# A fused RWKV-7 / RG-LRU / mixture-of-experts layer on one core: another order at the start of a scan pass, and smaller transfers

## The chip, the cores and the metric

The kernel runs on one core of a Trainium2 chip. The metric is the device time of one execution in microseconds (us). A TensorE matmul and its weight load appear in the profile as PE and PEld; DVE is VectorE, ACT ScalarE, POOL GpSimd and SP SyncE.

## The reference

One layer of a diffusion backbone on 2048 latent tokens and 256 context tokens of width 1024. After a modulated norm and one input projection, two mixers run in both directions over the tokens: a gated linear recurrence (RG-LRU) and the RWKV-7 recurrence with 8 heads of 64, whose step is

```python
sa = jnp.einsum('bhvk,bhk->bhv', s, -kk_t)
s = (s * w_t[:, :, None, :] + sa[..., None] * (kk_t * a_t)[:, :, None, :]
     + v_t[..., None] * k_t[:, :, None, :])
return s, jnp.einsum('bhvk,bhk->bhv', s, r_t)
```

Their outputs are merged and projected, and a mixture of 16 experts and a last norm follow. The change touches only the stage that computes the two recurrences.

## The kernel before

The kernel is a row of stages: `entry` and `inward` (norm, input projection, operands of the recurrences), `scan` (both recurrences), `blend`, `outward`, `choose`, `experts`, `final`. In fp32 they each write their results to scratch tensors in DRAM.

`scan` works through 18 passes of 128 positions per direction in 64-wide chunks. Two units `u` (0 and 1) of 128 partitions each carry the heads, both directions `d` side by side. A pass of the RWKV recurrence has two parts. The *solve* (argument `a`) forms, for all chunks of pass `it`, the products of the operands and inverts a triangular matrix by five levels of squaring. The *state* part (argument `c`) carries the state S through the four chunks of the pass before, chunk by chunk in steps X, Z, S and Y. `body(a, c)` interleaves both on every engine in a fixed order: five steps `begin0` to `begin4`, then for each level m a step F and a step W; `STATE_AT` says which state step stands behind which solve step (X of chunk 0 behind `begin0`, Z0 behind `begin1`, S0 and Y0 behind `begin2`, X1 behind `begin3`, Z1 behind `begin4`, S1 and Y1 behind F1, and so on). There is no scheduler: each engine runs its queue in this order, and semaphores (`Steps`: one per engine and unit, counted by name) hold it where it needs another's result.

The five steps of the solve before the change, on PE: `begin0` makes L and its transpose Lt for both units, from `ob` and `aq` (L2273), into PSUM banks 2 and 3. `begin1` and `begin2` are `joint`: products B of one unit and K of the other at once (L2288), into the same banks. `begin3` transposes operands, tB, and V, out of `ob` and `over`, with an identity; `begin4` does tK. ACT copies L, tB, V and tK out of PSUM (L2430, L2433, L2435, L2438); DVE masks Lt into T (L2599) and B and K into W, Lb, La and Lk, a direction at a time (L2607); POOL adds units to T and W (`start_solve`, L2774) and masks L into the tiles H of the levels (`level`, L2784). F1 multiplies H with W.

The same queues carry the RG-LRU, a piece of 256 positions per chunk: ACT's `gates` behind X, at Z the `squares` and, at chunk 0, `roots` of four pieces (L2535, with a table load before and behind), `window` behind Y; DVE's `series` (L2663 to L2668), `taps` and `gated_input` (L2652, L2658), and `recur` (L2674 to L2693) behind S of chunks 0 and 2; POOL's `squares` (L2792). POOL also sums the modulation rows (`add`, `wm`) at the end of each of the first 16 passes.

Loads of the operands: SP's `reload(it)` waits for tK of pass `it` and then loads `ob` and `over` for the next pass, single buffers (L2225 to L2227). `aq` has two buffers and is loaded by `reload_own` when the state part has ended; the stores of `y` follow (L2246).

## Time and profile before

| | |
|---|---|
| median of 3 runs | 4309.09 us (4306.44 to 4311.71) |
| the profiled execution, its own time | 4309.31 us, span 4307.5 us |
| busy: PE, PEld, DVE, ACT, POOL | 3596.5, 3199.9, 2432.9, 1889.2, 1258.8 us |
| scan stage | about 1117 to 2395 us |
| queue q8 (instruction): packets, MB | 411, 6.73 |
| DMA issues of the scan, KB each | `over` 512, `ob` 256, `aq` 516, `y` 64, `wm` (all_late<-in_w_mod) 512, `raw` 1024 and 128 |

A row of a group, wait or timeline names line, engine, operation and out<-in by the names of tiles; "scan_b" is the PSUM. Each fp32 matmul of the program shows as two records. "issue" as the one that ended an idle time means that the profile names nothing that the engine waited for. Queue q1 carries SP's transfers, q10 ACT's, q0 POOL's, q8 and q14 instructions.

### The profile page before, as it was taken

The numbers are of one execution on the slowest core, as the hardware profiler recorded it, in microseconds if no ns is written. First come the engines' busy times: TensorE is split into PE (matmuls) and PEld (weight loads), VectorE is DVE, ScalarE is ACT, GpSimd is POOL, SyncE is SP. The second block draws the span as 40 slices with busy tenths as digits, with TensorE's granted clock in tenths as the row PEclk, the third lists the DMA queues.
The fourth block names the chain that finished last, engine by engine and source line by source line (L and its number), as shares of the span: only waits on it lengthen the run. The fifth ranks groups of instructions, "written<-read, shape, count | busy, mean of one in ns | idle before, by whom it ended". The sixth has DMA issues, their size and how long they took to land. (4 is left out here: it accounts for less than half of the span.)

```text
span 4307.5 us, 117683 instructions
## 1 busy us (share of the span) xinstructions
PE 3596.5 (83%) x50061; PEld 3199.9 (74%) x50061; DVE 2432.9 (56%) x4389; ACT 1889.2 (44%) x3285; POOL 1258.8 (29%) x1250
## 2 busy tenths in 40 slices
PE   5799999999677777877777588894599999999992
PEld 2678888888577676777667488672499999999992
DVE  3237676510156666677767654435666666666664
ACT  3246665521154555555555443331244444444444
POOL 2223333311254655555553254000001010101110
PEclk8899999999898999999999799996699999999996
DMA  5235555532433333332331574431367676767675
GB/s 173 69 127 180 170 185 168 171 111 71 117 72 83 93 82 83 83 92 79 87 96 35 175 229 142 147 127 40 115 196 221 195 219 198 214 203 209 208 207 196
DMA packets 566343, 610.18 MB, mean 142 GB/s; under 512 B 65938, under 2 KB 471252, under 8 KB 564820
## 3 DMA queue, kind: packets, MB, share of 16 engines
q1 hardware_dynamic: 515540, 487.01, 36.9%
q0 software_dynamic: 21536, 76.56, 6.2%
q10 hardware_dynamic: 28768, 39.16, 2.8%
q8 instruction: 411, 6.73, 0.6%
q14 instruction: 88, 0.72, 0.1%
HBM read 443.09 MB, written 159.40 MB: 140 GB/s over the span
## 5 line engine op out<-in xcount | busy, mean ns | idle before, releaser
L339 DVE TENSOR_TENSOR moe_w_lo<-moe_w_lo_whole,moe_w_hi 128x2048 fp32r<-128x2048 f32 (+1 forms) x258 | 453.6, 1758 | 263.5 <-ACT moe_w_hi L517 188.0
L460 PE MATMUL moe_h<-moe_xt_hi,moe_w_hi 128*128 128x256 f32 x2048 | 582.0, 284 | 15.9 <-DVE moe_xt_lo L339 14.8
L460 PE MATMUL moe_h<-moe_xt_lo,moe_w_hi 128*128 128x256 f32 x2048 | 580.1, 283 | 0.6 <-issue 0.6
L460 PE MATMUL moe_h<-moe_xt_hi,moe_w_lo 128*128 128x256 f32 x2048 | 580.1, 283 | 0.0
L1792 PE MATMUL inward_pp<-u_u_hi,inward_w_hi 128*128 128x512 f32 (+1 forms) x1360 | 527.4, 388 | 20.8 <-POOL inward_w_lo L1952 20.8
L1792 PE MATMUL inward_pp<-u_u_lo,inward_w_hi 128*128 128x512 f32 (+1 forms) x1360 | 515.7, 379 | 0.0
L1792 PE MATMUL inward_pp<-u_u_hi,inward_w_lo 128*128 128x512 f32 (+1 forms) x1360 | 515.5, 379 | 0.0
L460 PEld LDWEIGHTS moe_h<-moe_xt_hi,moe_w_hi 128*128 128x128 f32 x2048 | 393.2, 192 | 27.9 <-issue 23.7
L460 PEld LDWEIGHTS moe_h<-moe_xt_lo,moe_w_hi 128*128 128x128 f32 x2048 | 393.3, 192 | 3.7
L460 PEld LDWEIGHTS moe_h<-moe_xt_hi,moe_w_lo 128*128 128x128 f32 x2048 | 393.3, 192 | 1.1 <-issue 0.8
L412 POOL DMA_INDIRECT scratch_x<-moe_ys,moe_who x32 | 70.6, 2205 | 912.2 <-DVE moe_ys L568 907.4
L1792 PEld LDWEIGHTS inward_pp<-u_u_hi,inward_w_hi 128*128 128x128 f32 x1360 | 257.1, 189 | 80.1 <-POOL inward_w_lo L1952 21.0
L1792 PEld LDWEIGHTS inward_pp<-u_u_hi,inward_w_lo 128*128 128x128 f32 x1360 | 257.0, 189 | 48.8
L1792 PEld LDWEIGHTS inward_pp<-u_u_lo,inward_w_hi 128*128 128x128 f32 x1360 | 257.4, 189 | 46.3
L2273 PE MATMUL scan_b<-scan_F,scan_T 64*64 64x64 f32 x5760 | 218.2, 228 | 61.4 <-issue 55.2
L2273 PE MATMUL scan_b<-scan_W,scan_H 64*64 64x64 f32 x5760 | 212.6, 227 | 52.0 <-issue 35.1
L1916 ACT ACTIVATE inward_out<-inward_pp 128x512 f32<-128x512 f32 (+1 forms) x170 | 97.6, 577 | 354.7 <-PE inward_pp L1792 353.7
L2273 PEld LDWEIGHTS scan_b<-scan_F,scan_T 64*64 64x64 f32 x5760 | 196.5, 141 | 76.2 <-issue 68.4
L503 ACT ACTIVATE moe_w_hi<-moe_w_lo_whole 128x2048 fp32r<-128x2048 f32 x128 | 243.4, 1901 | 0.1
L2273 PEld LDWEIGHTS scan_b<-scan_W,scan_H 64*64 64x64 f32 x5760 | 193.9, 141 | 65.0 <-issue 64.2
L2784 POOL TENSOR_TENSOR scan_H<-scan_L,scan_masks 128x512 f32<-128x512 f32 x180 | 237.9, 1351 | 4.5 <-PE scan_b L2273 4.5
L517 ACT ACTIVATE moe_w_hi<-moe_w_lo_whole 128x1024 fp32r<-128x1024 f32 x128 | 135.6, 1060 | 223.8 <-PE moe_y L443 223.8
(374 smaller groups left out, 9832.1 us busy)
## 6 DMA issues: line engine op xcount, KB each, us to landing
moe_w_lo_whole<-in_moe_w SPq DMA_DIRECT2D x387, 512.0 KB, 5.0
scratch_ops<-inward_ops SPq DMA_DIRECT2D x72, 514.0 KB, 3.8
scan_over<-scratch_ops SPq DMA_DIRECT2D x72, 512.0 KB, 9.9
inward_w_lo_whole<-in_w_in SPq DMA_DIRECT2D x38, 512.0 KB, 4.6
scan_aq<-scratch_ops SPq DMA_DIRECT2D x36, 516.0 KB, 5.0
scratch_gates<-inward_out SPq DMA_DIRECT2D x64, 256.0 KB, 2.2
all_late<-in_w_mod POOLq DMA_DIRECT2D x32, 512.0 KB, 4.5
rest_modsum<-scratch_gates SPq DMA_DIRECT2D x64, 256.0 KB, 4.4
```

Of the source, the lines that this page charges most:

```text
L339: return nc.vector.tensor_tensor(x_lo, x, x_hi.bitcast(F32), ALU.subtract)
L412: pool.indirect_dma_start(env["x1"], bass.IndirectOffsetOnAxis(who[u][h][:, :], 0), ys[:, u, h, :], None, compute_op=ALU.add).then_inc(s_s ...
L460: mm = nc.tensor.matmul(hb[ft % 2][m][:, 0:CAP], w_, x, start=(k == 0 and part == 0), stop=(k == KD - 1 and part == 2))
L503: AC.did(f"{u}w13h{ft}", act.activation(w13_hi[:, to], w13[:, at], ACT.Copy))
L517: AC.did(f"{u}w2h{ft}", act.activation(w2_hi[:, to], w2[:, at], ACT.Copy))
L1792: mm = nc.tensor.matmul(pp[k % NB][:, 0:size], wx, ux, start=(kk_ == 0 and part == 0), stop=(kk_ == KD - 1 and part == 2))
L1916: act.activation(out[:, k % R, 0:size], pp[k % NB][:, 0:size], func).then_inc(s_ev, 1)
L2273: mm = nc.tensor.matmul(bank[u][to][other if across else h, k * HD:(k + 1) * HD], lhs(h, k), rhs(h, k), start=True, stop=True)
L2784: PO[u].did(f"H{m}", pool.tensor_tensor(four(H[u][(m - 1) % 3][:, :, :]), four(L[u][:, :, :]), masked(f"lev{m}t"), ALU.mult))
```

## The change

The solve's steps get another order: `begin0` is tB and V, `begin1` tK, `begin2` L and Lt, `begin3` and `begin4` the two joint products. ACT's and DVE's parts move with them. The waits follow: tB and V wait for `ob` and both halves of `over` and for the PSUM banks of the pass before; tK and L wait for ACT's copy of what stood in the bank; F1 waits for the DVE's last eviction of the second product. On POOL, `squares` of chunk 0 and H1 come ahead of T0 and W0.

SP's `reload` waits for the later of the joint products instead of tK, and loads `over` in eight pieces (a direction at a time) instead of four. `aq` is loaded a direction at a time as well, and each unit's `aq` and `y` transfers are issued as soon as that unit is done. `raw` is loaded in four pieces of its latents, two of them a piece of work later, and `wm` in two halves, each reloaded when it has been summed.

```diff
--- before.py
+++ after.py
@@ -2159,11 +2159,11 @@
 
-        PE = [Steps(n.sem(f"pe_solve{u}"), ["L", "Lt"] + list(FIRST_OF[u]) + ["tB", "V", "tK"] + level_pe) for u in U]
-        AC = steps("act_solve", ["L", "tB", "V", "tK"] + [f"F{m}" for m in LEVELS])
+        PE = [Steps(n.sem(f"pe_solve{u}"), ["tB", "V", "tK", "L", "Lt"] + list(FIRST_OF[u]) + level_pe) for u in U]
+        AC = steps("act_solve", ["tB", "V", "tK", "L"] + [f"F{m}" for m in LEVELS])
         DV = [Steps(n.sem(f"dve_solve{u}"), ["T0"] + [f"{x}{d}" for p in FIRST_OF[u] for x in EVICTED[p] for d in U] +
                     [f"{x}{m}" for m in LEVELS for x in "TW" if m < 5 or x == "W"]) for u in U]
-        PO = steps("pool_solve", ["T0", "W0"] + [f"H{m}" for m in LEVELS])
+        PO = steps("pool_solve", ["H1", "T0", "W0"] + [f"H{m}" for m in LEVELS[1:]])
         PEc = steps("pe_state", chunks(["X", "Z", "S", "Y"]))
...
@@ -2216,45 +2216,53 @@
         def _(sp):
-            def load(it, own, rest):
+            def own(it, u, d):
+                sp.dma_start(aq[u][:, it % 2, d, :], env["ops"][:, it][u][:, d, 2 * G:4 * G + 4]).then_inc(s_aq[u][it % 2], 16)
+
+            def load(it):
                 src = env["ops"][:, it]
                 for u in U:
-                    if own:
-                        sp.dma_start(aq[u][:, it % 2, :, :], src[u][:, :, 2 * G:4 * G + 4]).then_inc(s_aq[u][it % 2], 16)
-                    if rest:
-                        sp.dma_start(ob[u][:, :, :], src[u][:, :, 4 * G + 4:OPS]).then_inc(s_ob[u], 16)
-                        sp.dma_start(over[u][0:HD, :, :], src[u][HD:P, :, 0:4 * G]).then_inc(s_over0[u], 16)
-                        sp.dma_start(over[u][HD:P, :, :], src[u][0:HD, :, 0:4 * G]).then_inc(s_over1[u], 16)
+                    sp.dma_start(ob[u][:, :, :], src[u][:, :, 4 * G + 4:OPS]).then_inc(s_ob[u], 16)
+                for d in range(2):
+                    for u in U:
+                        sp.dma_start(over[u][0:HD, d, :], src[u][HD:P, d, 0:4 * G]).then_inc(s_over0[u], 16)
+                        sp.dma_start(over[u][HD:P, d, :], src[u][0:HD, d, 0:4 * G]).then_inc(s_over1[u], 16)
 
             def reload(it):
+                PE[0].wait(sp, "K", it)
+                PE[1].wait(sp, "B", it)
+                load(it + 1)
+
+            def store(it, u):
+                ACc[u].wait(sp, "Y3", it)
+                for d in range(2):
+                    for h in range(2):
+                        dst = env["y"][d, bass.ds(it, 1), :, u * P + h * HD:u * P + (h + 1) * HD].rearrange("o (c s) v -> s (o c) v", s=HD)
+                        sp.dma_start(dst, y[u][64 * h:64 * h + 64, 4 * d:4 * d + 4, :]).then_inc(s_y[u], 16)
+
+            def pass_end(it):
                 for u in U:
-                    PE[u].wait(sp, "tK", it)
-                load(it + 1, False, True)
-
-            def reload_own(it):
-                for u in U:
-                    PEc[u].wait(sp, "Y3", it)
-                    DVc[u].wait(sp, "Sb3", it)
-                load(it + 2, True, False)
-
-            def store(it):
-                for u in U:
-                    ACc[u].wait(sp, "Y3", it)
-                    for d in range(2):
-                        for h in range(2):
-                            dst = env["y"][d, bass.ds(it, 1), :, u * P + h * HD:u * P + (h + 1) * HD].rearrange("o (c s) v -> s (o c) v", s=HD)
-                            sp.dma_start(dst, y[u][64 * h:64 * h + 64, 4 * d:4 * d + 4, :]).then_inc(s_y[u], 16)
+                    if it + 2 <= LAST:
+                        PEc[u].wait(sp, "Y3", it)
+                        DVc[u].wait(sp, "Sb3", it)
+                        for d in range(2):
+                            own(it + 2, u, d)
+                    store(it, u)
 
             n_main = sum(k for _, k in CONST_SIZES)
-            load(0, True, True)
+            load(0)
+            for u in U:
+                for d in range(2):
+                    own(0, u, d)
             sp.dma_start(masks[:, :], t["consts"][:, n_main:n_main + len(MASKS) * P]).then_inc(s_masks, 16)
-            load(1, True, False)
+            for u in U:
+                for d in range(2):
+                    own(1, u, d)
             reload(0)
             for it in range(LAST + 1):
                 if it + 2 <= LAST:
                     reload(it + 1)
-                    reload_own(it)
-                store(it)
+                pass_end(it)
             for u in U:
@@ -2290,15 +2298,13 @@
                 it, b, half = a
-                uB, uK = (0, 1) if r == 1 else (1, 0)
+                uB, uK = (0, 1) if r == 3 else (1, 0)
                 for u in U:
-                    if r == 1:
+                    if r == 3:
                         AC[u].wait(pe, "L", it)
                         DV[u].wait(pe, "T0", it)
                     else:
                         DV[u].wait(pe, EVICTED[FIRST_OF[u][0]][1] + "1", it)
-                pe.wait_ge(s_over0[uK], 16 * it + 16)
-                pe.wait_ge(s_over1[uK], 16 * it + 16)
                 for k in range(8):
@@ -2310,18 +2316,20 @@
                 if r == 0:
-                    pe.wait_ge(s_aq[u][b], half * 16 + 16)
                     pe.wait_ge(s_ob[u], 16 * it + 16)
+                    pe.wait_ge(s_over0[u], 32 * it + 32)
+                    pe.wait_ge(s_over1[u], 32 * it + 32)
                     DV[u].wait(pe, "W5", it - 1)
-                    two(u, ("L", 2, oA, oB), ("Lt", 3, oA, oB))
-                elif r == 3:
-                    DV[u].wait(pe, second_done[u], it)
                     two(u, ("tB", 2, oB, unit), ("V", 3, xV, unit))
-                else:
+                elif r == 1:
                     AC[u].wait(pe, "tB", it)
                     for k in range(8):
                         mm = one(u, 2, xK, unit, True, k)
                     PE[u].did("tK", mm)
+                else:
+                    pe.wait_ge(s_aq[u][b], half * 32 + 32)
+                    AC[u].wait(pe, "tK", it)
+                    two(u, ("L", 2, oA, oB), ("Lt", 3, oA, oB))
 
@@ -2330,7 +2338,7 @@
                     PO[u].wait(pe, "W0", it)
-                    AC[u].wait(pe, "V", it)
+                    DV[u].wait(pe, second_done[u], it)
                 for k in range(8):
...
@@ -2424,16 +2432,16 @@
                 it, b, _ = a
-                if r == 0:
+                if r == 2:
                     PE[u].wait(act, "L", it)
                     PO[u].wait(act, "H5", it - 1)
                     AC[u].did("L", act.activation(flat(L[u][:, :, :]), bank[u][2][:, :], ACT.Copy))
-                elif r == 3:
+                elif r == 0:
                     PE[u].wait(act, "tB", it)
                     AC[u].did("tB", act.activation(flat(tB[u][b][:, :, :]), bank[u][2][:, :], ACT.Copy, scale=-1.0))
                     PE[u].wait(act, "V", it)
                     AC[u].did("V", act.activation(flat(V[u][b][:, :, :]), bank[u][3][:, :], ACT.Copy))
-                elif r == 4:
+                elif r == 1:
                     PE[u].wait(act, "tK", it)
@@ -2459,7 +2467,8 @@
                 else:
-                    act.dma_start(raw[:, CTX:], src[:, LAT0:LAT0 + SEQ]).then_inc(s_lat, 16)
+                    n_ = SEQ // 4
+                    act.dma_start(raw[:, CTX + part * n_:CTX + (part + 1) * n_], src[:, LAT0 + part * n_:LAT0 + (part + 1) * n_]).then_inc(s_lat, 16)
 
...
@@ -2500,7 +2509,11 @@
                 elif k % (2 * NG) == 2 * NG - 1 and j + 1 < NJ:
-                    load_raw(j + 1, "latents")
+                    for part_ in range(2):
+                        load_raw(j + 1, part_)
+                elif k % (2 * NG) == 0 and k:
+                    for part_ in range(2, 4):
+                        load_raw(j, part_)
 
...
@@ -2594,11 +2608,11 @@
                 D = DV[u]
-                if r == 0:
+                if r == 2:
                     PE[u].wait(dve, "Lt", it)
                     D.did("T0", dve.tensor_tensor(four(T[u][:, :, :]), banked(bank[u][3]), masked("lev0t"), ALU.mult))
-                elif r in (1, 2):
-                    product = FIRST_OF[u][r - 1]
+                elif r in (3, 4):
+                    product = FIRST_OF[u][r - 3]
                     PE[u].wait(dve, product, it)
@@ -2746,16 +2760,17 @@
 
-            def load(part_):
+            def load(part_, x):
                 if part_ < 4 * KD:
-                    at, half = part_ // 2, part_ % 2
-                    pool.dma_start(wm, w_mod[:, NJ * half:NJ * (half + 1), 2 * D + at * G:2 * D + (at + 1) * G]).then_inc(s_wm, 16)
+                    at, k = part_ // 2, NJ * (part_ % 2) + NJ // 2 * x
+                    pool.dma_start(wm[:, NJ // 2 * x:NJ // 2 * (x + 1), :], w_mod[:, k:k + NJ // 2, 2 * D + at * G:2 * D + (at + 1) * G]).then_inc(s_wm[x], 16)
 
             def add(part_, count):
                 at, half = part_ // 2, part_ % 2
                 dst = env["modsum"][:, at * G:(at + 1) * G]
-                pool.wait_ge(s_wm, 16 * (part_ + 1))
                 for k in range(NJ):
+                    if k % (NJ // 2) == 0:
+                        pool.wait_ge(s_wm[k // (NJ // 2)], 16 * (part_ + 1))
                     to = part if half or k else dst
@@ -2764,10 +2779,12 @@
                         pool.wait_ge(s_sum, count)
-                load(part_ + 1)
+                    if k % (NJ // 2) == NJ // 2 - 1:
+                        load(part_ + 1, k // (NJ // 2))
                 return count
 
             def start_solve(it):
+                level(1, it)
                 for u in U:
@@ -2796,15 +2813,15 @@
             pool.wait_ge(s_masks, 16)
-            load(0)
+            for x in range(2):
+                load(0, x)
             count = 0
             for it in range(LAST + 2):
                 more, first = it <= LAST, 4 * (it - 1)
+                squares(first)
                 if more:
                     start_solve(it)
-                squares(first)
                 if more:
-                    level(1, it)
                     level(2, it)
```

## Rows read from the trace of the kernel before

**Rows 1.** Waits of PE, 1192 to 2299 us: total, times, longest.

```profile
PE scan_b L2273 <- issue: 134.8, 91, 7.0
PE scan_b L2288 <- issue: 38.4, 16, 2.4
PE scan_b L2383 <- DVE scan_Z L2633: 29.3, 14, 3.3
```

**Rows 2.** Timeline of PE: start, duration, and idle time before in brackets.

```profile
1438.02 0.26 PE L2273 MATMUL scan_b<-scan_T,scan_F 64*64 64x64 f32 x1 [7.04 <-issue]
...
1470.84 2.60 PE L2273 MATMUL scan_b<-scan_ob,scan_aq 64*64 64x64 f32 x115 [2.37 <-issue]
```

**Rows 3.** DMA queues, 1427 to 1435 us: packets, MB, share of 16 engines.

```profile
q1 hardware_dynamic: 678, 1.73, 103.3%
```

**Rows 4.** DMA queues, 1440 to 1460 us.

```profile
q8 instruction: 5, 0.08, 1.6%
```

**Rows 5.** DMA queues, 1169 to 1174 us.

```profile
q8 instruction: 1, 0.02, 1.7%
```

**Rows 6.** PE in 16 windows on the bursts, first and last: busy, matmuls, clock.

```profile
1219.00:1232.00 13.00, 6.94 (x233) 0.74 0.77 162
...
2258.00:2271.00 13.00, 7.71 (x262) 0.87 0.69 147
```

**Rows 7.** PE in the 16 windows behind them, first and last.

```profile
1233.00:1246.00 13.00, 11.58 (x474) 1.00 0.01 4
...
2272.00:2285.00 13.00, 10.84 (x489) 1.00 0.04 10
```

**Rows 8.** DMA issues: count, size, median time to landing.

```profile
scan_over<-scratch_ops SPq DMA_DIRECT2D x72, 512.0 KB, 9.9
```

**Rows 9.** Timeline of PE in one pass, 1543 to 1570 us.

```profile
1543.66 2.25 PE L2273 MATMUL scan_b<-scan_ob,scan_aq 64*64 64x64 f32 x122
...
1548.12 0.33 PE L2288 MATMUL scan_b<-scan_over 64*64 64x128 f32 x2
...
1553.33 0.33 PE L2288 MATMUL scan_b<-scan_aq,scan_ob 64*64 64x128 f32 x2 [2.42 <-issue]
...
1563.53 1.57 PE L2273 MATMUL scan_b<-all_consts,scan_over 64*64 64x64 f32 x48
...
1569.28 0.34 PE L2383 MATMUL scan_b<-scan_V,scan_tK 64*64 64x64 f32 x4 [1.59 <-DVE scan_Z L2633]
```

**Rows 10.** Timeline of ACT in the same pass.

```profile
1547.84 0.28 ACT L2448 ACTIVATE scan_X<-scan_b 128x128 f32<-128x128 f32 x1 [1.32 <-PE scan_b L2374]
...
1550.24 1.28 ACT L2535 ACT_TABLE_LOAD   x1
...
1555.44 0.59 ACT L2529 ACTIVATE scan_root<-all_late,scan_lc 128x256 f32<-128x256 f32 x1
...
1560.92 0.58 ACT L2433 ACTIVATE scan_tB<-scan_b 128x512 f32<-128x512 f32 x1
...
1562.35 0.60 ACT L2435 ACTIVATE scan_V<-scan_b 128x512 f32<-128x512 f32 x1
```

**Rows 11.** Timeline of DVE in the same pass.

```profile
1550.49 0.76 DVE L2607 TENSOR_TENSOR scan_W<-scan_b,scan_masks 128x256 f32<-128x256 f32 x2 [2.12 <-PE scan_b L2288]
...
1552.49 0.75 DVE L2607 TENSOR_TENSOR scan_Lk<-scan_b,scan_masks 128x256 f32<-128x256 f32 x2
...
1560.20 0.41 DVE L2674 SCALAR_TENSOR_TENSOR scan_root<-scan_gated,scan_root 128x256 f32<-128x256 f32 x1
...
1562.16 1.42 DVE L2674 SCALAR_TENSOR_TENSOR scan_root<-scan_gated,scan_root 128x256 f32<-128x256 f32 x1
...
1565.30 1.53 DVE L2693 TENSOR_TENSOR all_late<-all_late,scan_root 128x256 f32<-128x256 f32 x1
```

**Rows 12.** Timeline of POOL in the same pass.

```profile
1558.93 1.27 POOL L2774 TENSOR_TENSOR scan_W<-scan_W,all_consts 128x512 f32<-128x512 f32 x1 [4.14 <-DVE scan_W L2607]
```

**Rows 13.** Timeline of DVE in the first pass.

```profile
1142.29 1.29 DVE L2599 TENSOR_TENSOR scan_T<-scan_b,scan_masks 128x512 f32<-128x512 f32 x2 [23.42 <-DMA scan_masks<-in_consts]
```

More of the change, by code:

```diff
@@ L2178, in scan @@
         s_masks, s_sum, s_zero = n.sem("masks_loaded"), n.sem("mod_summed"), n.sem("state_zero")
-        s_wm = n.sem("wm_loaded")
+        s_wm = [n.sem(f"wm_loaded{x}") for x in range(2)]
         block = ctx.enter_context(nc.Block())
@@ L2400, in body @@
                 for r in range(5):
-                    if a is not None and r in (1, 2):
+                    if a is not None and r in (3, 4):
                         joint(r, a)
@@ L2476, in window @@
                 else:
-                    act.wait_ge(s_lat, 16 * (j + 1))
+                    act.wait_ge(s_lat, 64 * (j + 1))
                 if k:
@@ L2583, in _ @@
             load_raw(0, "context")
-            load_raw(0, "latents")
+            for part_ in range(4):
+                load_raw(0, part_)
             act.wait_ge(s_zero, 3)
```

## The prediction

> **What bounds the kernel now.** The scan stage is the stretch from about 1117 to 2395 us. I read first the waits of TensorE (PE) over sixteen of its passes, 1192 to 2299 us [rows 1]. PE waits there 134.8 us before L2273 and 38.4 us before the joint products for nothing that the profile names, and 29.3 us for the copy of Z; a pass lasts 69.2 us (1107/16). So PE, with its small matmuls in a fixed order, sets the pace of the scan, and what it loses falls in two kinds: waits inside the order of steps, and unnamed stalls.
>
> The 38.4 us are of the first kind: 16 times 2.42 us, in which the second joint product waits for VectorE (DVE) to mask the first one out of PSUM [rows 9, 11]. The unnamed stalls are of the second kind. The timeline of PE shows them in each pass, 10 to 15 us after SyncE reissues `ob` and `over`, here one of 7.04 us, and a smaller one, 2.37 us, after `aq` and `y` [rows 2]. The DMA views say what is late. In a quiet stretch a 16 KB packet of queue q8 (instructions) starts five times in 20 us, one per 4 us [rows 4]. In 1427 to 1435 us only q1 moved anything, 1.73 MB, and not one q8 packet started [rows 3]; PE stood still until 1438.02. I read this as PE's instruction fetch waiting behind the load burst. The price: in sixteen stretches laid on the bursts (210 us in all) PE executes 4,076 matmuls and is busy for 123.4 us [rows 6]; in the sixteen equally long ones just behind them it executes 7,547 and is busy for 186.1 us [rows 7]. By busy time a burst costs 62.7/16 = 3.9 us, by matmuls 210 x (1 - 4076/7547)/16 = 6.0 us, the granted clock being lower too (0.83 in the mean against 0.96).
>
> **Part 1: the pieces.** `over` goes from four transfers of 512 KB to eight of 256 KB a pass, `aq` from two of 516 KB to four of 258 KB; `ob` (256 KB) and `y` (64 KB) stay, and so do the bytes [rows 8]. A transfer spread on 16 engines puts 32 KB on each, now 16 KB. If a fetch waits for the transfer that its engine is at, and for one already taken, the wait halves with the piece. `over` is 2.0 of the 2.5 MB of the burst. I take half of 6.0 us: 3.0 us a pass. The `aq`/`y` stall of 2.37 us shrinks less, since the eight stores are unchanged: 0.8 us. Bounds: nothing at all, and all of it (6.0 + 2.4 = 8.4 us). 17 passes have such a burst: -3.8 x 17 = -65 us, between 0 and -143. By the Trainium skill (DMA: Bandwidth & Descriptors, Queues, rings and completion order) an engine takes turns between its queues one packet of 9 to 17 descriptors at a time; by that a fetch waits for one share at most, 2.4 us at the burst's 211 GB/s, and 1.2 us after the change; with two fetches a burst the saving would be 2.4 us a pass, -41 us. The wait of 8 us and more in rows 3 is longer than that rule gives.
>
> The issues: SyncE issues 10 loads instead of 6 at the reload (0.6 us each, +2.4 us) and 12 instead of 10 transfers at the pass end. It only waits otherwise, the loads are needed 45 us later, and `y` is rewritten some 20 us later: nothing. Without that cover it would be 3.6 us a pass. GpSimd (POOL) issues two `wm` loads a part instead of one (0.8 us more, twice a pass), but each half is requested earlier, and no other engine needs the sum: nothing, and less DMA wait on POOL. ScalarE issues four `raw` pieces instead of one, three times in the kernel, a piece of work ahead of use: nothing. The reload now waits for the second joint product instead of `tK`; both end about 22 us into a pass, so the burst stays where it is.
>
> **Part 2: the order.** All matmuls stay. I replay the first steps of one pass, which begins at 1543.5 (L at 1543.66, 2.25 us for both units) and reaches the S step of chunk 1 at 1569.28, 25.8 us later [rows 9]. Durations: tB with V 2.2 us (as many matmuls as L), X 1.5, tK 1.6, joint product 2.3 (from 1548.1 to the 1550.49 at which DVE takes it), Z 0.7, S with Y 2.8, F1 1.2 a unit; ScalarE's four copies of tB and V 2.0 us, its X group 2.4 (1547.84 to 1550.24), square roots and squares with two table loads 5.8 (1550.24 to 1556.03) [rows 10]; DVE's eight evictions 2.75 us (1550.49 to 1553.24) [rows 11].
> New order, from 0. PE: tB and V to 2.2, X0 to 3.7. ScalarE: copies to 3.5, X group to 6.0, tK copies to 7.1. PE: tK to 5.2, Z0 to 5.8, then L, which now waits for tK to leave its bank (6.6): idle 0.9. L to 8.9, S and Y to 11.6. ScalarE's queue is what is late next: before L's copy now stand the roots and squares of chunk 0, 7.1 to 12.9, so L is copied by 14.0, and the first joint product starts at 14.1: idle 2.5. It ends at 16.4, X1 at 17.9. DVE: between the S copies and the evictions now stand two `recur` groups. They took 1560.20 to 1562.3 and 1562.16 to 1566.8 (2.1 and 4.7 us), the second beside POOL's H tiles [rows 11]. From 11.8 they end between 14.5 and 18.4. Evictions then end between 19.3 and 21.1, and the second joint product runs from there: idle 1.5 to 3, where 2.42 was. Behind its end (21.7 to 23.5) F1 of unit 0 now waits for two evictions (1.4 us, 0.7 of it under Z1), and F1 of unit 1 for POOL's W0, which has its W one eviction later and takes 1.27 us [rows 12]: together idle 1.8. S1 starts between 26.5 and 28.3, and no longer waits for the copy of Z (1.59 us here, 29.3/16 = 1.8 us a pass). Against 25.8: +0.7 to +2.5. I take +1.5 us: +25 us over 17 passes. Bounds: -0.5 (the stalls of 0.6 us before X0 and X1 vanish in the new idle time) and +3.5.
>
> **Part 3: the first pass, once.** There T0 waited for `masks` until 1142.29 [rows 13]. tB, V and tK now come ahead of that wait. They cost 2.2 + 1.6 = 3.8 us behind it: -4 us. The bytes ahead of `masks` are about as before.
>
> **Sum.** -65 + 25 - 4 = -44 us. The profiled execution took 4309.31 us (span 4307.5), the median of the runs is 4309.09: 4265 us.
>
> **Rivals.** *The wait goes by what is queued, not by the piece.* All bytes of the burst are requested within 7 us, before and after. For it: in rows 3 the fetch starts only near the burst's end. Against it: in 1169 to 1174 a q8 packet started amid the burst of an earlier pass [rows 5]. Then only parts 2 and 3 are left, 4330 us: slower. The Trainium skill (Runtime: NRT & Kernel Launch, Instruction fetch mechanics) says that the fetch of the next 16 KiB block is mostly hidden by the pace of issue; by that there is no stall to shorten either. The 7.04 us of rows 2 speak against it.
> *The fetch hardly waits any more.* If halved pieces let it in before PE runs dry, four fifths of the 143 us go: -114 + 21, 4216 us. For it: outside the bursts PE keeps going with a packet each 4 us, so a short delay may be covered.
> *The other side: DVE's `recur` ahead of the evictions.* If both groups run at the slow 4.7 us beside POOL's T0, W0 and H tiles in each pass, the evictions slip by another 3.9 us: 5.4 x 17 = 92 us, and with the fetch's gain 92 - 65 - 4 = +23, 4332 us. It decides from 4.1 us a pass on. For it: one of two groups is slow in rows 11; against it: the slow one lay under four H tiles, of which two now come later.
> *The change does not do what it says*: order and pieces cancel (3.8 against about 3.8 a pass), 4309 us.
>
> **How the numbers follow.** The forecast (4235 to 4300) 0.48; the queue rival 0.20; the near-full gain 0.14; the `recur` rival 0.12; cancelled 0.06. A difference under 0.2% (8.6 us) could hardly be told from none. Faster: 0.48 + 0.14 = 0.62; same: 0.06 and 0.03 from the edges of the slower cases: 0.09; slower 0.29. The range 4200 to 4335 holds the forecast, most of the near-full gain and both slower cases at their centres; outside stay the halves beyond them (some 0.2).
>
> **What would show it.** The unnamed stall 10 to 15 us after the reload at about half of 5 to 7 us, and q8 packets starting within the burst (part 1); if it stays, the queue rival holds. Idle PE before the first joint product of about 2.5 us, and before F1 (part 2); the Z copy gone from PE's waits; L copied behind the roots. The first F1 at about 1156 instead of 1160 (part 3). I am wrong if the burst's stall is not the fetch, or if DVE is later than replayed.

## The result, and the profile after

The changed kernel takes 4329.65 us in the median of 7 runs (4318.2 to 4347.95), the kernel before 4307.6 us (4304.7 to 4311.71): ratio 1.0057, 95% interval 1.0039 to 1.0075. It is slower by 22 us, where 44 us less were forecast. The profiled execution has a span of 4327.9 us, 20.4 more than before. The first thing to read is where these 20.4 us lie. Rows of PE in three windows, the stages scan, blend and experts, laid from a stage's first instruction to its last (the columns: window, its length, PE busy and its matmuls, granted clock, DMA share, GB/s). Before:

```profile
1117.70:2401.00 1283.30, 949.38 (x33984) 0.92 0.33 83
2406.00:2687.00 281.00, 229.54 (x1704) 0.90 0.65 203
3062.90:4235.80 1172.90, 1131.45 (x7952) 0.99 0.67 203
```

After:

```profile
1118.40:2396.80 1278.40, 945.16 (x33984) 0.93 0.32 83
2402.00:2687.50 285.50, 233.52 (x1704) 0.89 0.64 200
3064.70:4257.10 1192.40, 1137.23 (x7952) 0.98 0.66 200
```

The scan, the only stage whose code changed, is 4.9 us shorter: order and pieces all but cancel. (The same scan differs by 12 to 14 us from one profile to the next, see runs 1, 2, 5, 6 and 12, so 4.9 us is no gain that can be told from none.) `experts`, whose code is the same and which begins some 665 us later, is 19.5 us longer. That is nearly all of the difference; `blend` has 4.5 us, the stages between the rest.

Waits of PE in the scan after, 1190 to 2290 us (total, times, longest), to be read beside [rows 1]:

```profile
PE scan_b L2281 <- issue: 133.7, 101, 4.8
PE scan_b L2296 <- DVE scan_Lk L2621: 25.7, 16, 3.8
PE scan_b L2281 <- DVE scan_Lk L2621: 22.7, 16, 1.9
PE scan_b L2296 <- ACT scan_L L2438: 16.1, 14, 1.7
PE scan_b L2281 <- DVE scan_W L2640: 11.1, 23, 0.6
PE scan_b L2281 <- POOL scan_W L2791: 10.3, 14, 0.8
```

The wait for the copy of Z is gone, as foreseen. In its place stand PE's waits for L's copy before the first joint product, for DVE's last eviction before the second (L2296) and before F1 (L2281), and for W0 of POOL. The longest unnamed stall fell from 7.0 to 4.8 us. The sum of those before L2273, now L2281, hardly fell: 134.8 to 133.7 us. The timeline of PE in one pass after, answering to [rows 9]; the pass begins at 1532.17 and S1 starts at 1560.99:

```profile
1540.96 2.08 PE L2281 MATMUL scan_b<-scan_ob,scan_aq 64*64 64x64 f32 x126 [0.47 <-ACT scan_tK L2446]
...
1548.33 0.33 PE L2296 MATMUL scan_b<-scan_aq,scan_ob 64*64 64x128 f32 x2 [1.33 <-ACT scan_L L2438]
...
1553.32 0.33 PE L2296 MATMUL scan_b<-scan_aq,scan_ob 64*64 64x128 f32 x2 [1.21 <-DVE scan_Lk L2621]
...
1557.68 1.49 PE L2281 MATMUL scan_b<-scan_W,scan_H 64*64 64x64 f32 x32 [1.93 <-DVE scan_Lk L2621]
...
1559.64 1.65 PE L2281 MATMUL scan_b<-scan_W,scan_H 64*64 64x64 f32 x26 [0.47 <-POOL scan_W L2791]
```

Every wait that the replay of part 2 named is here. The DMA queues in a burst after, 1275 to 1286 us, answering to [rows 3] (packets, MB, share of 16 engines):

```profile
q1 hardware_dynamic: 1153, 2.55, 88.5%
...
scan_over<-scratch_ops SPq DMA_DIRECT2D x8, 256.0 KB, 6.1
```

Again no q8 packet starts until the burst is over (one at 1274.68, the next at 1286.16), and PE stands 3.94 us until 1288.83. So with half the piece the interval between two q8 packets did not shrink here; in the changed kernel the longest one over each of the sixteen reloads is 10.3 us in the mean, against 8.9 before. The first F1 of the first pass starts at 1155.35, against some 1160 before, as forecast in part 3.

### The profile page after: what moved, and what is told of

Same layout as the page of the kernel before. It is cut to its first block and busy times, and to the rows that moved or that the text cites. A ratio compares the mean times of both kernels' runs of the same rounds, so it can differ in the third digit from the quotient of the medians.

```text
span 4327.9 us, 117870 instructions
## 1 busy us (share of the span) xinstructions
PE 3605.8 (83%) x50061; PEld 3201.6 (74%) x50061; DVE 2417.2 (56%) x4389; ACT 1890.4 (44%) x3285; POOL 1264.1 (29%) x1282
## 5 line engine op out<-in xcount | busy, mean ns | idle before, releaser
L460 PE MATMUL moe_h<-moe_xt_hi,moe_w_hi 128*128 128x256 f32 x2048 | 584.2, 285 | 15.9 <-DVE moe_xt_lo L339 15.1
L460 PE MATMUL moe_h<-moe_xt_hi,moe_w_lo 128*128 128x256 f32 x2048 | 583.7, 285 | 14.8 <-issue 14.8
L460 PE MATMUL moe_h<-moe_xt_lo,moe_w_hi 128*128 128x256 f32 x2048 | 582.9, 285 | 0.0
L460 PEld LDWEIGHTS moe_h<-moe_xt_hi,moe_w_hi 128*128 128x128 f32 x2048 | 396.1, 193 | 27.3 <-issue 23.6
L460 PEld LDWEIGHTS moe_h<-moe_xt_hi,moe_w_lo 128*128 128x128 f32 x2048 | 396.2, 193 | 16.2 <-issue 16.2
L460 PEld LDWEIGHTS moe_h<-moe_xt_lo,moe_w_hi 128*128 128x128 f32 x2048 | 396.0, 193 | 3.7
L2281 PE MATMUL scan_b<-scan_W,scan_H 64*64 64x64 f32 x5760 | 220.1, 231 | 76.8 <-DVE scan_Lk L2621 26.5
L2281 PEld LDWEIGHTS scan_b<-scan_W,scan_H 64*64 64x64 f32 x5760 | 200.4, 144 | 89.7 <-issue 75.5
L2281 PE MATMUL scan_b<-scan_F,scan_T 64*64 64x64 f32 x5760 | 213.5, 226 | 52.6 <-issue 45.0
L2281 PEld LDWEIGHTS scan_b<-scan_F,scan_T 64*64 64x64 f32 x5760 | 191.6, 138 | 63.5 <-issue 54.0
```

The source lines that it names most:

```text
L460: mm = nc.tensor.matmul(hb[ft % 2][m][:, 0:CAP], w_, x, start=(k == 0 and part == 0), stop=(k == KD - 1 and part == 2))
L2281: mm = nc.tensor.matmul(bank[u][to][other if across else h, k * HD:(k + 1) * HD], lhs(h, k), rhs(h, k), start=True, stop=True)
```

## The experiments

The first theory (A): the scan gained about what it lost, and the loss arises in `experts` from the place at which its loop stands in PE's instructions, since the new order's waits are 35 more semaphore instructions on PE ahead of it (1445 in place of 1410). The rival (B): data, buffers or DMA left by the scan slow `experts`. Within the scan the disputed numbers are the prices of order and of pieces, and whether the piece or the queued bytes decide (the queue rival of the prediction).

**1 and 2. Empty instructions.** At the end of PE's queue in the scan:

```diff
             through(pe, body)
+            for _ in range(35):     # 221 in the changed kernel
+                pe.nop()
```

> The kernel before, with 35 empty instructions at the end of PE's queue of the scan, where PE waits for nobody and DVE ends 10 us later. The changed kernel has 35 more semaphore instructions on PE than the kernel before, and its experts stage, whose code is the same, took 1192.4 us instead of 1172.9, with an unnamed stall of about 2 us once in each turn of the loop. Theory A (place of the loop in PE's instruction stream): the same shift alone gives the same stalls, +15 to +20 us, about 4325 us, all of it in experts. Theory B (the experts stage was only slow by chance, or by what the scan leaves behind): no change, 4308 us.

> The changed kernel with 221 empty instructions at the end of PE's queue of the scan, so that the experts loop stands 256 instructions further than in the kernel before, that is at the same place within a block of 256 (16 KB, the size of a q8 packet). Theory A: the stalls in the experts loop go, -15 to -20 us against the changed kernel, about 4308 us or a little less than the kernel before, since the scan was 5 us shorter. Theory B: no difference from the changed kernel, 4330 us.

Measured: 4304.27 us, ratio 0.9998 (0.9986 to 1.0011), and 4326.36 us, 1.0054 (1.0039 to 1.0069). PE had as many instructions as without them, so the empty ones were not in the program; these are a repeat of either kernel. They say nothing on A, and they repeat the stages: scan 1279.4 and 1285.1 us, `experts` 1172.7 and 1192.1 us. `experts` repeats within half a microsecond. The scan does not: in the profiles of its old form (before, runs 1, 5, 12) it takes 1279.4 to 1291.8 us, in those of its changed form (after, runs 2, 6) 1271.6 to 1285.1. A difference between two single scans is good to some 10 us.

**3. The pieces alone.** The old order of the solve with all the transfers of the change:

```diff
-    sp.dma_start(over[u][0:HD, :, :], src[u][HD:P, :, 0:4 * G])
+    for d in range(2): sp.dma_start(over[u][0:HD, d, :], src[u][HD:P, d, 0:4 * G])
```

> The kernel before with the change's transfers alone: over, aq, raw and wm in pieces, each unit's aq and y issued when it is done; the order of the steps is the old one, and PE has as many instructions as before. By my prediction: -65 us, 4245 us. By the queue rival: no change at the reload. What the changed kernel's trace suggests: the q8 interval over the reload stays (8.8 us before, 10.0 after), the one at the pass end falls from 6.1 to 5.1 us; so -1 us a pass, about 4290 us.

Measured: 4261.33 us (4258.03 to 4268.66), ratio 0.9909 (0.9893 to 0.9924), 44 us faster. All of it lies in the scan:

```profile
1116.70:2352.20 1235.50, 941.29 (x33984) 0.93 0.33 86
```

That is 47.8 us less; `experts` stays at 1173.5 us. The gain lies between the two that were expected (65 and some 15 us): the changed transfers, taken alone, are a good change.

**4. The order alone**, with the old transfers (and 221 empty instructions, without effect as in run 2).

> The changed order of the steps with the transfers as they were (whole over and aq, raw and wm in one), and 221 empty instructions on PE behind the scan, so that the experts loop is where it was. By my prediction: +25 - 4 = +21 us, 4329 us. If the order costs nothing, as the scan of the changed kernel (1278.4 us against 1283.3) allows: 4308 us or, with 4 us of the first pass, 4304 us.

Measured: 4367.25 us (4355.45 to 4368.04), ratio 1.0142 (1.0123 to 1.0162), 62 us slower: the scan takes 1319.0 us (+35.7), `experts` 1193.9 us (+21.0). Both expected times (4329 and 4304 to 4308) were too low. So the order costs twice: in its stage and again in a later stage.

**5 and 6. Instructions that are really there.** Semaphore increments at the same place; 35 in the kernel before (as many as the change adds), 221 in the changed kernel, which makes 256 in all:

```diff
             through(pe, body)
+            for _ in range(35):     # 221 in the changed kernel
+                n.apart(pe)
```

> The empty instructions of the first try did not reach the program (PE's instruction counts in the trace are those without them), so that it tested nothing. Now the kernel before with 35 increments of a semaphore nobody waits for, at the end of PE's queue of the scan: PE's program is as long as the changed kernel's. Theory A (the place of the loop in the instruction stream costs the experts stage its 20 us): experts 1192 instead of 1173 us, 4325 us. Theory B (something else of the new order costs it): 1173 us, 4306 us.

> The changed kernel with 221 such increments: the experts loop stands exactly 256 instructions (16 KB) behind its place in the kernel before. Theory A: experts back at 1173 us, 4308 us. Theory B: 1192 us, 4328 us.

Measured: the kernel before goes to 4324.49 us, ratio 1.0043 (1.0026 to 1.0059), as theory A wanted it. The changed kernel is at 4316.27 us, 1.0046 (1.0025 to 1.0067) of before, where 4308 was expected, but with the time of its increments in it: the last instruction of the scan ends 23.8 us before `blend` begins, against 5.3 us before. The whole time alone can't tell it from the changed kernel (1.0057), so the stage decides. `experts` in run 5, then in run 6:

```profile
3074.10:4266.70 1192.60, 1137.37 (x7952) 0.98 0.66 200
```

```profile
3068.70:4244.10 1175.40, 1130.85 (x7952) 0.99 0.67 202
```

The old scan with 35 increments has the slow `experts`, the changed scan moved on to 256 has all but the fast one. B falls: in run 5 data, buffers and transfers are those of before. Over all profiles `experts` takes 1192.1 to 1195.8 us with 35 more instructions on PE ahead of it (after, runs 2, 4, 5, 9) and 1172.7 to 1174.2 us with none (before, runs 1, 3, 7, 8, 10, 11). The idle time ahead of the matmuls of L460 that ended with "issue" (total, times) is, in the order before, after, run 5, run 6:

```profile
  issue: 25.1, 29
```

```profile
  issue: 54.5, 38
```

```profile
  issue: 54.4, 38
```

```profile
  issue: 32.5, 32
```

The timeline of PE shows what it is. After, in the second turn of the loop, and then run 5:

```profile
3233.12 0.28 PE L460 MATMUL moe_h<-moe_xt_lo,moe_w_hi 128*128 128x256 f32 x1
3235.79 0.39 PE L460 MATMUL moe_h<-moe_xt_hi,moe_w_lo 128*128 128x256 f32 x1 [2.38 <-issue]
```

```profile
3244.50 0.39 PE L460 MATMUL moe_h<-moe_xt_hi,moe_w_lo 128*128 128x256 f32 x1 [1.68 <-issue]
```

`experts` is a loop of eight turns (L427) with a branch back at the end of each:

```profile
L427 PEldq COMPARE_BRANCH  x8: 83/3428/3514, 3226.6 to 4244.6; - x8
```

A taken branch occupies the sequencer for 3.3 to 3.9 us, in every kernel, while PE still works off what is queued. Seven times, once behind each taken branch, the changed kernel then stops for 1.6 to 2.6 us, always 73 records of PE and PEld behind the branch (some 33 of them belong to the turn before and were queued); run 5 stops at the same record. The waits of PE in `experts` after, 3065 to 4257 us, have these seven stops:

```profile
PE moe_h L460 <- issue: 14.8, 7, 2.6
```

With 5.8 us more of busy time on PE (1137.23 against 1131.45 us, granted clock 0.98 against 0.99) they make up the 19.5 us. Run 6 passes that record and stops 34 records further on, in three turns of seven, for 1.1 to 1.6 us. The DMA rows of the second turn say what PE waits for. In the changed kernel one q8 packet starts at 3227.66 and the next only at 3232.71; from 3228 to 3232.6 there is only

```profile
q1 hardware_dynamic: 1891, 0.96, 69.2%
```

and PE runs dry at 3233.4. In the kernel before the two packets start at 3226.22 and 3231.6, just as far apart; PE is at its 73rd record at 3231.8 and at the 108th at 3234.0, and does not stop. In the seven turns of each of these two kernels the second packet starts 5.0 to 5.6 us after the first, and 35 instructions of the loop (2.2 us of PE's time) decide if PE has work until it has landed. The three turns in which run 6 stops are those in which its second packet is late, 6.5 to 7.2 us after the first; in the four others it is 5.1 to 5.5. The Trainium skill (Runtime: NRT & Kernel Launch, Instruction fetch mechanics) states that a taken branch to a place outside what is held forces a fetch of that block before execution goes on. The trace agrees: the first q8 packet starts 1.04 us after the branch at 3226.62, and the branch ends after 3.5 us.

**7. `over` in 128 KB pieces**, on run 3: each transfer cut once more, in 16 a pass.

```diff
+    for c in range(2):
+        cut = slice(2 * G * c, 2 * G * c + 2 * G)
-    sp.dma_start(over[u][0:HD, d, :], src[u][HD:P, d, 0:4 * G])
+        sp.dma_start(over[u][0:HD, d, cut], src[u][HD:P, d, cut])
```

> The old order with the change's transfers (4261 us), and over in 16 pieces of 128 KB instead of 8 of 256 KB. If PE's instruction fetch waits for the piece at hand, the long intervals between q8 packets (the sixteen longest 8.8 us with whole transfers, some 6.7 with 256 KB) fall again by half of what is above 4.1 us, to about 5.4, and the time by another 15 to 25 us, 4240 us. If the gain came from issuing aq and y unit by unit, or from raw and wm, no change: 4261 us.

Measured: 4221.67 us (4210.72 to 4225.19), ratio 0.9802 (0.9784 to 0.9819); the scan takes

```profile
1117.80:2312.40 1194.60, 927.30 (x33984) 0.94 0.33 89
```

another 40.9 us less, where 15 to 25 were expected. The bytes and the queue are the same, but not the time in which they are asked for. SyncE issues a transfer every 0.64 us, so by the issues and landings in the trace a reload of before is requested within 4.4 us in the mean, that of run 3 within 7.4 and this one within 13.8, and a piece lands 8.4, 6.8 and 3.6 us (medians) after its issue. Size and backlog of the transfers fall together, so run 7 can't separate the two. In a burst of this kernel, 1207 to 1222 us, three q8 packets start amid q1's:

```profile
q1 hardware_dynamic: 1739, 2.49, 61.8%
q8 instruction: 3, 0.05, 1.6%
```

The starts of q8 between 1190 and 2300 us, worked out from the trace, lie about 4 us apart in quiet stretches in each kernel. The longest interval over each of the sixteen reloads is 8.9 us in the mean before (15 above 7 us), 6.6 us in run 3 (5 above 7), and 5.1 us here (none).

**8. One piece at a time.** Run 3, but behind each piece of `ob` and `over` SyncE waits until it has landed before it issues the next of any tile, so that one alone is outstanding. The pieces are those of run 3.

```diff
     sp.dma_start(over[u][0:HD, d, :], ...).then_inc(s_over0[u], 16)
+    if it: sp.wait_ge(s_over0[u], 32 * it + 16 * d + 16)
```

> As with the change's transfers in the old order (4261 us), but SyncE waits for each piece of ob and over to land before it issues the next, so that only one is ever queued. 10 pieces of about 3.5 us take 35 us, less than the 47 until they are needed. If the fetch waits for what is queued, the long q8 intervals go (5 us or less) and the time falls by 25 to 40 us, 4230 us. If it waits for the piece at hand alone, little changes: 4255 us. If the loads come too late: slower than 4261 us.

Measured: 4261.89 us (4249.79 to 4278.77), ratio 0.9903 (0.988 to 0.9926), the scan 1236.1 us. The time is that of run 3, but it is made up otherwise. Waits of PE, 1189 to 2290 us, in run 3, then in run 8:

```profile
PE scan_b L2281 <- issue: 125.4, 105, 4.0
PE scan_b L2281 <- DMA scan_aq<-scratch_ops: 1.5, 3, 1.1
```

```profile
PE scan_b L2287 <- issue: 82.7, 89, 2.9
PE scan_b L2287 <- DMA scan_aq<-scratch_ops: 45.4, 22, 4.5
PE scan_b L2302 <- DMA scan_over<-scratch_ops: 5.8, 1, 5.8
```

The unnamed stalls fell by 43 us with pieces of the same size, below those of run 11, which has hardly any bytes in the reload (93.4 us there). The longest q8 interval over a reload fell from 6.6 to 5.5 us in the mean, none above 6.5; the five still above 7 us that carry load bytes lie beside `aq` and `y`, which are not held back. What was won is lost again because the reload now takes 36.5 us in the mean, from the first issue to the last landing (14.2 in run 3), and `aq`, issued behind it, comes late. So what stands queued with the piece does matter, and the size of the piece is not shown to matter by itself: the expected 4230 us for "the fetch waits for what is queued" was missed because of `aq`.

**9. The new order with 128 KB pieces**, the changed kernel with run 7's cut.

> The changed kernel with over cut once more, into sixteen pieces of 128 KB a pass (the new order stays). Theory: the order's cost (some 35 us in the scan, some 20 us in experts) and the pieces' gain are separate terms. Then the second halving gives about what it gave in the old order (e3 to e7: 40 us), reduced as the first halving was (37 of 48): 30 to 40 us, so 4290 to 4300 us, ratio to before 0.996 to 0.999, and experts still near 1192 us. Rival: the order's own waits lie in the burst and hide the fetch, so that smaller pieces win little more: within 10 us of the changed kernel, 4320 to 4330 us, ratio 1.003 to 1.006.

Measured: 4287.16 us (4278.06 to 4304.52), ratio 0.9961 (0.9946 to 0.9975), a little less than the 4290 to 4300 us expected; `experts` takes 1195.8 us. The scan:

```profile
1116.20:2347.20 1231.00, 922.23 (x33984) 0.96 0.31 86
```

36.4 us longer than in run 7, where run 4 had 35.7 over the kernel before and the changed kernel has 42.9 over run 3: within the scatter the order's price is the same whatever the pieces. The longest q8 interval over a reload is 7.5 us in the mean here, against 5.1 in run 7. Its waits, 1189 to 2290 us:

```profile
PE scan_b L2298 <- DVE scan_Lk L2623: 30.3, 17, 3.8
PE scan_b L2283 <- DVE scan_Lk L2623: 24.1, 17, 1.9
PE scan_b L2298 <- ACT scan_L L2440: 16.6, 17, 2.0
PE scan_b L2283 <- POOL scan_W L2793: 11.9, 15, 0.8
```

**10 and 11. Smaller still, and no bytes.** Run 10 has `over` in 32 pieces of 64 KB and `ob` in four of 128 KB. Run 11 is run 3 with 16 columns a transfer from the second pass on, so it leaves out most of the operands' loading (and computes with those of the first pass).

```diff
-    for c in range(2): cut = slice(2 * G * c, 2 * G * c + 2 * G)
+    for c in range(4): cut = slice(G * c, G * (c + 1))
```

```diff
+    src, n_ = env["ops"][:, 0], 16 if it else 4 * G
-    sp.dma_start(over[u][0:HD, d, :], src[u][HD:P, d, 0:4 * G])
+    sp.dma_start(over[u][0:HD, d, 0:n_], src[u][HD:P, d, 0:n_])
```

> Old order, over in 32 pieces of 64 KB and ob in four of 128 KB a pass (36 issues at a reload, some 22 us of SyncE's time). Theory (each fetch waits for the piece its engine is at): the longest q8 intervals go from some 5.5 us to between 4.1 (quiet) and 5 us, and the time falls by another 10 to 20 us against e7: 4200 to 4212 us, ratio 0.976 to 0.979. Rival: at 128 KB the fetch already keeps pace, nothing is left: 4215 to 4230 us, ratio 0.98. Third: SyncE's issues are late for the next pass, or the more descriptors hold the fetch again: slower than e7 by 10 us or more.

> Old order, the pieces of e3, but from the second pass on each ob and over transfer carries 16 columns only (8 KB to 16 KB instead of 256 KB) and all operands are those of the first pass; so this kernel leaves out the loading of most operands. Every PE instruction stays. It is the floor of what cutting the pieces can win. Theory: all of the stall behind the reload is the fetch waiting for these bytes; no PE stall of over 3 us is left there, the q8 intervals are near 4.1 us throughout, and the time is below e7: 4180 to 4210 us, ratio 0.971 to 0.978. Rival: the stall belongs to the instruction stream at this place (it would come without traffic): above 4240 us, ratio over 0.985.

Measured: 4222.74 us (4214.27 to 4233.1), ratio 0.9802 (0.9784 to 0.9819), and 4191.9 us (4184.19 to 4195.63), ratio 0.9731 (0.9717 to 0.9745). The scan in run 10, then in run 11:

```profile
1116.20:2320.10 1203.90, 931.55 (x33984) 0.94 0.34 88
```

```profile
1117.80:2283.30 1165.50, 915.98 (x33984) 0.95 0.21 54
```

Run 10 gives nothing over run 7, as the rival in its expectation said: its passes are as long (64.12 and 64.09 us), its first pass ends 8 us later, where the many issues stand ahead of the first step. Run 11 is the floor: without the bytes the scan is 117.8 us shorter than before, within the expected range, and the longest q8 interval over a reload is 4.5 us in the mean. The transfers of run 3 win 47.8 of these (0.41), those of run 7 88.7 (0.75).

**12. Twice the shift.** The kernel before with 70 increments (the diff of run 5 with 70), to see whether the stall in `experts` has a fixed price or one by distance.

> The kernel before with 70 semaphore increments at the end of PE's scan queue, twice the 35 of e5. In the changed kernel and in e5 PE stops in each turn of the experts loop 73 records behind the branch at L427 for about 2.1 us; in the kernel before it passes that place, and 35 records take it 2.2 us (3231.8 to 3234.0). Theory: PE reaches the end of the first fetched block before the second has come, so what is lost is a matter of how many instructions of the loop lie in the first block: with 70 the stall comes 38 records behind the branch, lasts about 4.2 us in each of seven turns, and the experts stage goes from 1173 to about 1205 to 1212 us; with blend and scan as in e5 the time is 4340 to 4350 us, ratio 1.008 to 1.011. Rival: a fixed price of a loop that starts in another place, whatever the distance: stalls of about 2 us, experts at 1192 us, 4325 to 4330 us, ratio 1.004 to 1.005.

Measured: 4353.27 us (4346.7 to 4359.13), ratio 1.0103 (1.0085 to 1.0121). The scan is at 1281.4 us as before; `experts`:

```profile
3060.60:4275.40 1214.80, 1142.39 (x7952) 0.97 0.65 196
```

+41.9 us for 70 instructions, after +19.7 for 35, where 32 to 39 were expected. PE stops in all seven turns, now 39 records behind the branch, for 4.4 to 5.2 us. In the second turn:

```profile
3231.47 0.55 PE L460 MATMUL moe_h<-moe_xt_hi,moe_w_hi 128*128 128x256 f32 x1 [4.86 <-DVE moe_ys L568]
```

The profile puts the stop down to DVE's `moe_ys`. In the kernel before, the same wait of PE is passed at 3229.58, before DVE's writes of that turn that raise the semaphore (3230.71 on), so PE doesn't need them: it is the wait instruction itself that is late. The fixed price falls, the distance holds.

## Why the prediction was wrong

**The step that failed first is the sum: it has no term for any stage but the scan.** "-65 + 25 - 4" is a sum over one stage, and the 35 waits that the new order adds on PE stand in it at nothing. Shown (runs 5, 6 and 12): they move the loop of `experts` in PE's instruction stream, and this costs 19.5 us of the 20.4. Without it the change would have made next to no difference (+0.9 us of the 20.4); that it would not have been faster either is due to the next two.

**Part 1, the pieces: the stall is read rightly, the term mis-sized, the law behind it not shown.** Forecast -65, measured -47.8 in the old order (run 3) and 1319.0 - 1278.4 = -40.6 in the new. That the stall is PE's fetch behind the bursts is shown: it shrinks as the transfers are cut (runs 3, 7), goes with the bytes (run 11), and the q8 intervals shorten with it in the old order. That it goes by the piece at hand, as the part assumed, is not shown, and run 8 speaks against it: with the same pieces, one at a time, the unnamed stalls fell by 43 us. Cutting also spreads the requests out (4.4, 7.4, 13.8 us), so the gain of runs 3 and 7 can be that of a smaller backlog. No run has whole transfers one at a time, or small pieces all queued at once. The price by matmuls, 6.0 us a burst or 102 us in all, was the right one to take (117.8 measured); "the wait halves with the piece" was a little too much (0.41), and the 0.8 us for `aq` has no evidence of its own. That it wins 7 us less in the new order lies within the scatter of the scan.

The estimate of -41 us from the Trainium skill's share of one packet (DMA: Bandwidth & Descriptors, Queues, rings and completion order) was nearer than mine in the sum. But by that estimate a fetch waits at most 2.4 us before the change; the packets lay up to 12.1 us apart there, where quiet ones lie about 4, so the measurements are against it and the sum was luck. The near-full gain lies at run 7, not at the change.

**Part 2, the order: the waits foreseen, the sum mis-sized.** Forecast +25 with +1.5 us a pass; measured +2.1 (35.7/17), within the bounds. In the pass shown S1 starts 28.8 us after its begin, later than the 26.5 to 28.3 forecast. In the mean of sixteen passes of run 4 the new named waits are 5.0 us (3.1 for DVE's evictions, 0.8 L's copy, 0.8 W0, 0.3 tK's copy), less than the 6.7 to 8.2 replayed; gone are the Z copy's 1.8 and the 2.4 before the second product. What the replay got wrong is the other side: "the stalls of 0.6 us before X0 and X1 vanish in the new idle time". They did not: in the pass shown PE still stands 1.59 us for nothing named in the midst of X0, until 1537.10; and the unnamed ones together rose from 10.8 to 11.8 us a pass, and PE's busy time by 1.0 us (966.0 against 949.4 us, clock 0.91 against 0.92). The `recur` rival did not come: in the pass shown the two groups took 4.6 us together and ended at 1550.6, with the evictions at once behind them. (The replay's early end for them, 14.5, is too early even by its own rows: two groups of 2.1 us from 11.8 end at 16.0. The first joint product ends at 16.4, so the sum is the same.)

**Part 3** is right in number: the second pass begins 3.8 us earlier with the change, and in run 4, the order alone, the first F1 comes 3.5 us earlier. But in run 3, the old order, it comes 3.8 us earlier too; the order and the transfers each give these 4 us, and together they give them once.

**Costed at nothing:** the issues of SyncE, POOL and ScalarE. Right at ten loads a reload (run 3) and at 18 (run 7); at 36 the first pass pays 8 us.

**The rivals.** The queue rival gave 4330 us, a hit by number that was luck: it priced the pieces at nothing, and run 3 is 44 us faster. Its premise, that all bytes are requested within 7 us before and after, hid that the time of the requests grows (4.4 us before, 6.6 after); its law, that the wait goes by what is queued, is the one that run 8 supports. "Order and pieces cancel" is what the scan did (-4.9 us), and it had 0.06.

The sum as measured, by the profiled executions: order +35.7, pieces -40.6, `experts` +19.5, `blend` and the short stages around it +5.8: +20.4 us. Open stays `blend`: from its first to its last instruction 281.0 to 284.6 us in the five kernels with 35 more PE instructions, 279.5 to 281.4 in the others, runs 6 and 12 among them. Its place may matter too; nothing here separates that from scatter. Open stays too why the q8 intervals over a reload are longer in the new order (10.3 us against 6.6 in run 3, 11.6 in run 4 against 8.9 before) and PE's unnamed stalls, those of the second joint product apart, 1 us a pass longer (11.8 against 10.8 in run 4, 10.7 against 9.7 in the changed kernel and run 3). PE then waits for others within the burst and may ask for its next block at another time; no run tests it.

## What to carry to other kernels

When the engine that sets the pace issues many small instructions, count as a cost of each load burst the time that its instruction fetch stands behind it; cut the loads to pieces (here 128 KB: -82 us, and no more from 64 KB), or spread their requests where nothing behind them in the same queue is urgent, and leave the order alone unless a wait on the pacing engine falls by more than the new ones add. And when an edit adds or drops instructions on an engine, read every later loop of that engine in the profile, a few dozen records behind its branch: a few increments or waits more or less may be worth more than the edit. The version to keep is run 7, the old order with small pieces.

## What the hardware showed unexpectedly

A loop's turn on PE costs twice. The taken branch takes 3.3 to 3.9 us, hidden here by queued matmuls; and the q8 packet behind the first one starts 5.0 to 5.6 us after it (up to 7.2 in run 6), so that PE stops if it reaches the end of the first block sooner: 0 us in the kernel before, about 2.1 us with 35 instructions less in that block, 4.9 us with 70 less, seven times each.

A q8 packet takes 0.9 to 1.6 us on its engine in the kernel before, but its start is held up beside a burst of loads: in the old order the longest interval over a reload is 12.1 us with whole transfers, 8.1 with pieces of 256 KB, 5.9 with 128 KB, and 6.5 with 256 KB one at a time. In the new order it is 13.9, 13.2 and 10.6 us with whole transfers, 256 KB and 128 KB, so the piece alone doesn't set it. (All worked out from the starts of the packets.)
